# One block for norm, input projection and S5 in a hybrid Hyena, S5 and mixture-of-experts layer

## What is computed

```python
hc = modulate(rmsnorm(ctx, norm1_g[l]), csh1, csc1)
u_c = (hc @ w_in[l][:, HY_COLS:]).astype(jnp.float32)
stc_f, stc_b = s5_states(u_c, *s5_par, zero, zero)
init_f, init_b = stc_f[-1], stc_b[0]
...
h = modulate(rmsnorm(x, norm1_g[l]), sh1, sc1)
z = h @ w_in[l]
u = z[..., HY_COLS:].astype(jnp.float32)
st_f, st_b = s5_states(u, *s5_par, init_f, init_b)
y = jnp.concatenate([hyena_branch(z[..., :HY_COLS], rows, conv_w[l], conv_b[l], filt, hy_bias[l]),
                     s5_readout(u, st_f, st_b, *s5_out)], axis=-1)
x = x + g1[:, None] * (y.astype(x.dtype) @ w_out[l])
```

## Time and profile before

| | |
|---|---|
| median of 3 runs | 2789.76 us (2781.54 to 2794.0) |
| the profiled execution | 2789.57 us, span 2787.8 us |
| mean granted clock of TensorE | 0.926 |
| PE busy | 2440.3 us, 88% |
| DVE busy | 1901.2 us, 68% |
| ACT busy | 1312.9 us, 47% |
| POOL busy | 361.8 us, 13% |
| DMA | 716.41 MB, mean 257 GB/s |

### The profile page before, as it was taken

How to read it: one execution, slowest core, us unless ns; L and a number is a source line. 1 busy time by engine, 2 the same in 40 slices (tenths; PEclk the granted TensorE clock), 3 DMA queues, 4 the chain that set the end, 5 groups by cost and what they waited for, 6 DMA issues and landing times. The chain is left out here.

```text
span 2787.8 us, 27845 instructions
## 1 busy us (share of the span) xinstructions
PE 2440.3 (88%) x11074; PEld 1837.5 (66%) x11074; DVE 1901.2 (68%) x1293; ACT 1312.9 (47%) x778; POOL 361.8 (13%) x190
## 2 busy tenths in 40 slices
PE   7987499879786657749999999999999999999994
PEld 2333388633345536648888888888888888888883
DVE  4744433270729625488888888888888888888885
ACT  2111512000011122147767677777767676777673
POOL 0522300000000011000221022102201210221010
PEclk9989599999996679869999999999999999999997
DMA  7554311232235261459999999999999999999994
GB/s 255 205 191 162 99 46 31 102 117 91 90 83 120 55 204 61 172 190 360 374 368 373 378 376 371 374 373 369 380 371 375 367 376 374 379 363 376 378 363 187
DMA packets 174286, 716.41 MB, mean 257 GB/s; under 512 B 10626, under 2 KB 36130, under 8 KB 152405
## 3 DMA queue, kind: packets, MB, share of 16 engines
q1 hardware_dynamic: 167406, 689.82, 65.8%
q0 software_dynamic: 5184, 20.97, 2.8%
q10 hardware_dynamic: 1640, 4.85, 0.5%
HBM read 672.63 MB, written 42.98 MB: 257 GB/s over the span
## 5 line engine op out<-in xcount | busy, mean ns | idle before, releaser
L1819 DVE TENSOR_TENSOR w_low<-w_raw,w_high 128x4096 fp32r<-128x4096 f32 (+2 forms) x288 | 1164.0, 4064 | 93.9 <-ACT w_high L1784 93.9
L1784 ACT ACTIVATE w_high<-w_raw 128x4096 fp32r<-128x4096 f32 (+2 forms) x288 | 964.2, 3348 | 470.9 <-PE psum L1754 260.5
L1752 PE MATMUL psum<-w_high,x_high 128*128 128x512 f32 (+1 forms) x1536 | 578.4, 377 | 20.2 <-DVE w_low L1819 17.5
L1753 PE MATMUL psum<-w_low,x_high 128*128 128x512 f32 (+1 forms) x1536 | 573.8, 374 | 0.0
L1754 PE MATMUL psum<-w_high,x_low 128*128 128x512 f32 (+1 forms) x1536 | 572.1, 372 | 0.0
L1752 PEld LDWEIGHTS psum<-w_high,x_high 128*128 128x128 f32 x1536 | 290.1, 189 | 80.7 <-DVE w_low L1819 25.1
L1754 PEld LDWEIGHTS psum<-w_high,x_low 128*128 128x128 f32 x1536 | 289.3, 188 | 52.2
L1753 PEld LDWEIGHTS psum<-w_low,x_high 128*128 128x128 f32 x1536 | 289.9, 189 | 49.6
L1765 PE MATMUL psum<-w_high,a_high 128*128 128x512 f32 x704 | 220.9, 395 | 0.0
L1765 PE MATMUL psum<-w_low,a_high 128*128 128x512 f32 x704 | 217.5, 390 | 0.0
L1765 PE MATMUL psum<-w_high,a_low 128*128 128x512 f32 x704 | 217.1, 390 | 0.0
(11 more groups left out here) (321 smaller groups left out, 2835.9 us busy)
## 6 DMA issues: line engine op xcount, KB each, us to landing
w_raw<-in_ex_w_down SPq DMA_DIRECT2D x80, 2048.0 KB, 9.2
w_raw<-in_ex_w_gate SPq DMA_DIRECT2D x64, 2048.0 KB, 9.8
w_raw<-in_ex_w_up SPq DMA_DIRECT2D x64, 2048.0 KB, 10.5
w_raw<-in_ex_w_gate SPq DMA_DIRECT2D x32, 1536.0 KB, 10.3
w_raw<-in_ex_w_up SPq DMA_DIRECT2D x32, 1536.0 KB, 7.7
arena<-in_mod_w SPq DMA_DIRECT2D x24, 1024.0 KB, 7.0
w_raw<-in_ex_w_down SPq DMA_DIRECT2D x16, 1024.0 KB, 8.2
arena<-const_dft_filter SPq DMA_DIRECT2D x8, 1024.0 KB, 7.7
```

What stands on the lines that cost most here:

```text
L1752: nc.tensor.matmul(o, xt_h[:, x], h[:, f], start=kk == 0, stop=False)
L1753: nc.tensor.matmul(o, xt_h[:, x], l[:, f], start=False, stop=False)
L1784: nc.scalar.activation(high[n % NHI][:, 0:w], raw[n % NS][:, 0:w], ACT.Copy).then_inc(hi_done, 1)
L1819: nc.vector.tensor_tensor(low[n % NS][:, 0:w], raw[n % NS][:, 0:w], high[n % NHI][:, 0:w].bitcast(F32), ALU.subtract).then_inc(lo_done, 1)
```

## The change

`projection` and `s5` are replaced by one stage, `mix`, in one block. Work is cut into 36 units, one chunk by one span each; the S5 chunks 12 to 15 come first (their context spans at once, as soon as the two context tiles are there), then x1 (4 to 7), x2 (8 to 11) and v (0 to 3). Weights are loaded by chunk (512 KB, rows of 512 bytes) instead of by two chunks. Token tiles go in pairs through squares, roots and scaling, and the first five products stand between the transposes of the tokens. Four PSUM banks rotate over the units; banks 4 and 5 serve the token transposes, then the states and the turns, banks 6 and 7 the outputs. S5 has eight rounds of four columns: states of round q after unit 8 + 3q, its outputs after unit 13 + 3q. The S5 tables are reloaded in every round. The 16 turns of x1 and v follow single units; x1 and x2 go to DRAM scratch and are loaded again by `long_conv`, which also takes the broadcast rows over from `s5`. The first Fourier matrix is loaded at the end of `mix`. In `long_conv` the buffer `g` and some others lie at new addresses; the arithmetic is the same.

The diff, cut to its core:

```diff
-def projection(k):
+def mix(k):
...
+    NT, NX, NW, NZ = TOK // P, 5, 3, 3
+    NQ, A = 8, 2
+    C, G = 2 * A, 2 * A
+    chunks = [12, 13, 14, 15, 4, 5, 6, 7, 8, 9, 10, 11, 0, 1, 2, 3]
+    NCT = len(chunks)
+    units = [(n, s) for s in (2, 0, 1) for n in range(3)] + [(3, s) for s in (2, 0, 1)] + [(n, s) for n in range(4, NCT) for s in range(2)]
+    last_unit = [max(i for i, (x, _) in enumerate(units) if x == n) for n in range(NCT)]
+    ends = {i: n for n, i in enumerate(last_unit)}
+    ready = {2: 2, 0: 6, 1: NT}
+    turns = {i: [i - 15] for i in range(15, 23)}
+    turns.update({31: [8], 32: [9], 33: [10], 34: [11, 12], 35: [13, 14, 15]})
+    state_at = {8 + 3 * q: q for q in range(NQ)}
+    turn_unit = {m: i for i in turns for m in turns[i]}
+    states_done = {i: sum(s <= i for s in state_at) for i in range(len(units))}
+    turns_done = {q: sum(turn_unit[m] < i for m in turn_unit) for i, q in state_at.items()}
...
+    spans = [slice(0, 512), slice(512, 1024), slice(0, CTX)]
...
+            def put_inputs(n):
+                b = ubuf_of[n]
+                sp.wait_ge(conv, last_unit[n] + 1)
+                sp.dma_start(k.z_u[n * P:(n + 1) * P].rearrange("p s k -> p (s k)"), ubuf[b]).then_inc(uout[b], 16)
...
+            def in_tables(q):
+                if q:
+                    sp.wait_ge(smm, C * q)
+                else:
...
+                sp.dma_start(et.rearrange("p r d a n -> p (r d) (a n)"), t.rearrange("p r a n -> p r (a n)")).then_inc(tgot, 16)
...
+            def out_tables(q):
+                if q:
+                    sp.wait_ge(omm, q)
+                else:
+                    sp.wait_ge(mm, last_unit[2] + 2)
+                sp.dma_start(ot.rearrange("p r d a n -> p (r d) (a n)"), t.rearrange("p r a n -> p r (a n)")).then_inc(ogot, 16)
+                for w in range(2):
+                    for s in range(T):
+                        sp.dma_start(ll[NH * s:NH * s + NH, :, w, :], lsrc[w, :, A * q:A * q + A, (T - 1 - s) * NH:(T - 1 - s) * NH + P]).then_inc(ogot, 16)
+
+            def chunk_inputs(q):
+                if q >= 3:
+                    sp.wait_ge(omm, q - 2)
+                for s in range(T):
...
+                    sp.dma_start(uc[q % 3][NH * s:NH * s + NH, :, :], src[s, :, G * q:G * q + G, :]).then_inc(ugot[q % 3], 16)
...
+            def put_outputs(q):
+                sp.wait_ge(oev, q + 1)
+                for t in range(T):
+                    sp.dma_start(dst[t, :, G * q:G * q + G, :], ys[q % 2][NH * t:NH * t + NH, :, :]).then_inc(yput[q % 2], 16)
...
+            tokens(0)
+            tokens(1)
+            weights(0)
+            tokens(2)
+            tokens(3)
+            weights(1)
+            tokens(4)
+            weights(2)
+            for n in range(5, NT):
+                tokens(n)
+            in_tables(0)
+            for i in range(6, len(units)):
+                if i in ends and ends[i] + NW < NCT:
+                    weights(ends[i] + NW)
+                if i in ends and ends[i] < 4:
+                    put_inputs(ends[i])
+                if i == 8:
+                    sp.wait_ge(uout[0], 16)
+                    chunk_inputs(0)
+                    chunk_inputs(1)
+                if i == 9:
+                    out_tables(0)
+                if i == 11:
+                    sp.wait_ge(uout[1], 32)
+                    sp.wait_ge(uout[2], 16)
+                    chunk_inputs(2)
+                if i in state_at and state_at[i] + 1 < NQ:
+                    in_tables(state_at[i] + 1)
+                if i in output_at:
+                    q = output_at[i]
+                    if q + 3 < NQ:
+                        chunk_inputs(q + 3)
+                    if q + 1 < NQ:
+                        out_tables(q + 1)
+                    put_outputs(q)
+                if i in (17, 19, 21, 23):
+                    q = (i - 17) // 2
+                    sp.wait_ge(vev, 2 * q + 2)
+                    sp.dma_start(k.x1_d[:, :, q * P:(q + 1) * P], x1_out[:, q % 2]).then_inc(x1o[q], 16)
+                if i in (22, 24, 26, 28):
+                    q = (i - 22) // 2
+                    sp.wait_ge(conv, last_unit[8 + q] + 1)
+                    sp.dma_start(k.x2_d[:, q, :], z_t[:, (8 + q) % NZ, :]).then_inc(x2o[q], 16)
+            sp.dma_start(k.ring[:, 0, :], k.c["dft_signal"][0].rearrange("p m k n -> p (m k n)")).then_inc(pre, 16)
+            for q in range(HQ):
+                sp.wait_ge(x1o[q], 16)
+                sp.wait_ge(x2o[q], 16)
+            for b in range(2):
+                sp.wait_ge(yput[b], 16 * T * 4)
+            sp.wait_ge(pre, 16)
 
...
+            def turn_tokens(n):
                 pe.wait_ge(norm, n + 1)
                 if n >= 2:
                     pe.wait_ge(ev, n - 1)
                 for kk in range(KD):
...
+            def product(i):
+                n, s = units[i]
+                pe.wait_ge(wlo, n + 1)
+                pe.wait_ge(hlo, ready[s])
+                if i >= 4:
+                    pe.wait_ge(conv, i - 3)
...
                 last.then_inc(mm, 1)
...
+            def turn_channels(m):
+                n, r = 4 + m // 2 if m < 8 else 8 + m // 2, m % 2
+                pe.wait_ge(conv, last_unit[n] + 1)
+                pe.wait_ge(vev, m - 1 if m >= 13 else m)
+                pe.wait_ge(sev, C * NQ if m >= 11 else C * states_done[turn_unit[m]] - 1)
...
+            def states(q):
+                pe.wait_ge(tgot, 16 * (q + 1))
+                pe.wait_ge(ugot[q % 3], 16 * T * (q // 3 + 1))
+                if turns_done[q]:
+                    pe.wait_ge(vev, turns_done[q])
+                for c in range(C):
...
+                    if n >= 2:
+                        pe.wait_ge(sev, n - 1)
...
+            def outputs(q):
+                pe.wait_ge(ogot, 16 * (1 + 2 * T) * (q + 1))
+                pe.wait_ge(std, q + 1)
+                if q:
+                    pe.wait_ge(oev, q)
...
+                last.then_inc(omm, 1)
...
+            turn_tokens(0)
+            turn_tokens(1)
+            product(0)
+            turn_tokens(2)
+            product(1)
+            turn_tokens(3)
+            product(2)
+            turn_tokens(4)
+            turn_tokens(5)
+            product(3)
+            turn_tokens(6)
+            turn_tokens(7)
+            product(4)
+            turn_tokens(8)
+            turn_tokens(9)
+            for i in range(5, len(units)):
+                product(i)
+                if i in state_at:
+                    states(state_at[i])
+                if i in output_at:
+                    outputs(output_at[i])
+                for m in turns.get(i, []):
+                    turn_channels(m)
...
+            def high_part(n):
+                act.wait_ge(wgot[n % NW], 16 * (n // NW + 1))
+                if n >= NW:
+                    act.wait_ge(mm, last_unit[n - NW] + 1)
+                nc.scalar.activation(whigh[n % NW], wraw[n % NW], ACT.Copy).then_inc(whi, 1)
...
+            def middle(i):
+                n, s = units[i]
+                c = chunks[n]
+                act.wait_ge(mm, i + 1)
...
+                if 7 <= n < 11:
+                    act.wait_ge(vtr, 2 * (n - 6))
+                elif 11 <= n < 15:
+                    act.wait_ge(x2o[n - 11], 16)
+                elif n == 15:
+                    act.wait_ge(vtr, 10)
...
+            def states(q):
+                bre, bim = bu[q % 2]
+                if q >= 2:
+                    act.wait_ge(std, q - 1)
...
+                    act.wait_ge(smm, q * C + c + 1)
...
+            squares(0)
+            roots(0)
+            scaled(0)
+            scaled(1)
+            squares(1)
             high_part(0)
+            high_tile(0)
+            high_tile(1)
+            roots(1)
+            scaled(2)
+            scaled(3)
+            squares(2)
             high_part(1)
...
+            high_tile(2)
+            roots(2)
+            high_part(2)
+            high_tile(3)
+            scaled(4)
+            scaled(5)
+            squares(3)
...
+            for i in range(7, len(units)):
+                if i >= 12:
+                    middle(i)
+                if i - 1 in ends and ends[i - 1] + NW < NCT:
+                    high_part(ends[i - 1] + NW)
+                if i == 8:
+                    sines(1)
+                if i == 9:
+                    sines(2)
+                if i >= 11 and i - 11 in range(0, 15, 3):
+                    sines(3 + (i - 11) // 3)
+                if i in state_at:
+                    states(state_at[i])
+                if i in output_at:
+                    outputs(output_at[i])
+                for m in turns.get(i, []):
+                    if m >= 8:
+                        keep(m)
...
+            def low_part(n):
+                dve.wait_ge(whi, n + 1)
+                tt(wlow[n % NW], wraw[n % NW], whigh[n % NW].bitcast(F32), ALU.subtract).then_inc(wlo, 1)
...
+            def neighbours(i):
```

(77 more changed lines are left out.)

593 lines of the change are left out of this document (258 added, 335 removed).

## The result

The changed kernel takes **2706.8 us** (median of 4 runs, 2701.5 to 2709.6) beside 2789.7 us for the kernel before (median of 4): ratio 0.970, 95% interval 0.968 to 0.973. The forecast was 2711 with a range of 2690 to 2745. The profiled execution took 2701.5 us, span 2699.7; it is the fastest of its four, so the spans of the two profiles lie further apart (88.1 us) than the medians (82.9).

The account below looks back on a forecast made before the run. PE's queue plus the waits standing in it was taken as the bound of the new block: +86.8 us for the longer block, -165.5 for the S5 stage gone, -78.7 in all, from 2789.76 to 2711 us, range 2690 to 2745.

Parts of the forecast that it names:

- Startup: Token chain, early products and turns at PE's low clock: product(6) starts at 360.4 us, the block's first load being at 273.2.
- rival (e): Block start: products 0 to 3 at full clock, inputs sooner: -14 us, 2697, down to 2685; chance 0.14.
- The hole: PE waits 12 us ahead of states(0), at 388.9, for unit(8)'s write and then the first S5 input loads.
- States(0) and (1): DVE's chain and ACT's sines ahead of states(1) make PE wait; states(1) end at 415.2 us.
- The rounds: After states(1), PE's queue of products 130.6, states 29.5, outputs 48.2 and turns 7.8: 216.1 us, product(35) ends at 631.3.
- Rival (c): DVE and ACT pace the rounds through angles, sines and states: 3 us a round, 21 us, 2732; chance 0.14.
- What the matmuls cover: PE's matmuls (186 us) cover DVE's S5 work (124 us), and PE's own S5 work runs at full clock.
- (a): The SP queue paces the rounds, table loads at 0.8 us, 8 to land: +24 us, 2735; chance 0.15.
- Rival (b): SP queue paces the rounds at the old loads' full price, weights transfer ahead: +114 us, 2825; chance 0.04.
- rival (d): PE's clock doesn't hold among short matmuls; slower outputs and cold starts of units behind: +59 us, 2770; chance 0.05.
- ACT's tables: Table loads for Sin between Copy and Identity on ACT: bounds 0 and 20 us, taken as 0.
- The end: After product(35), 4.5 us of ends and a barrier of 0.9; with the matrix already loaded, the convolution starts at 636.7 us.

Follow-up runs that it names:

- e8: Changed kernel with products 0 to 4 behind the turns of all ten token tiles on PE, their copies behind DVE's evacuations: 2704.1 us.
- e2: Changed kernel with sines(q+3) moved behind the state copies of the same unit in ACT's queue: 2695.8 us.
- e9: Changed kernel with sines behind state copies, also sines(1) behind those of states(0), and first S5 input loads issued earlier, behind chunk 4's weights: 2683.3 us.
- e4: Changed kernel with six more linked 640-element instructions on DVE in each round (one product of turn_back repeated): 2733.6 us.
- e1: Changed kernel without the interleaving: all 36 products first, then the eight S5 rounds, sines behind the state copies: 2804.2 us.
- e3: Changed kernel with each s5_local load issued three times in rounds 0 to 6, the copies to unused places: 2773.0 us.
- e12: Changed kernel with each s5_local load issued twice in rounds 0 to 6: 2722.6 us.
- e11: Changed kernel without the early load of the first matrix, which the first convolution loads itself: 2710.0 us.

## Why the prediction was right, step by step

PE's queue with its waits added up as forecast where it counts most, in the rounds. The steps around them were off by up to 6.9 us, and part of that cancelled: the block was 6.9 us shorter than forecast, and the convolutions 2.0 us longer.

Counted from the first load (the prediction's times less 273.2, the measured ones less 270.2):

| step | forecast | measured |
|---|---|---|
| product(0) starts | 20.1 | 21.2 |
| product(3) starts | 59.6 | 54.5 |
| product(6) starts | 87.2 | 80.3 |
| products 6 to 8 | 16.3 | 16.6 |
| hole ahead of states(0) | 12.2 | 8.2 |
| states(0) to the end of states(1) | 26.3 | 29.1 |
| to the end of product(35) | 216.1 | 217.0 |
| to the first convolution | 5.4 | 5.4 |
| longer block | +86.8 | +79.9 |

- **Startup, 6.9 us too long.** The mis-sized term is the early products and turns. I priced products of 256 columns at 5.2 to 5.4 us, all at the low clock, and the turns behind them at 2.0. They took 4.4 to 4.6 and, behind products 0 and 1, 1.04. In product(0) the matmuls stand 0.21 us apart, then 0.12 from the middle of it on: the granted clock went from its lower level (1.2 GHz) to its upper (2.4 GHz) inside the product, and the turn behind it ran at the upper one. Product(6) came 6.9 us early, outside the 5 I had given. That is part of rival (e). e8 adds that these early products, which I followed step by step, have no effect on the end.
- **The hole, 4.0 us too long.** Write, loads and PE in series was the right mechanism. The size came from loads of 80 KB, 8.7 us from issue to PE; the new ones of 40 KB took 6.4 (368.87 to 375.27), and unit(8) was written 1.4 us after product(8) instead of 2.9. That PE falls to its low clock in it was right: states(0) took 5.1 us, at a granted clock of 0.58.
- **States(0) and (1), 2.8 us too short.** DVE's chain and the wait behind the sines were forecast, the wait was 5.1 us, and e2 confirms its cause. The chain itself, from turn_in to the end of the angles, took 18.5 us (18.8 forecast). The main term that was too small is the one put at nothing, the low clock in states(0): its copies were done 5.7 us after its start and not 3.6. In e9, where the hole is gone and states(0) ran at clock 1.00, they were done after 4.0. DVE's chain starts behind these copies, and PE waits for that chain in states(1), so PE was the late one there. The end of states(1) came 4.9 us after the angles, 3.9 forecast. States(0) in the windows view, the changed kernel and e9:

```profile
375.27:380.40 5.13, 5.13 (x49) 4.85 (x49) 0.00 (x0) 1.49 (x6) 0.00 (x0) 0.58 0.27 58
...
379.30:383.50 4.20, 4.03 (x54) 3.59 (x55) 3.96 (x9) 2.10 (x9) 0.00 (x0) 1.00 1.01 317
```

- **The rounds, right to 0.9 us in 217.** Eight outputs of 5.98 us (6.0), the clock at 0.99. Putting ACT's middle copy, high_part and sines onto PE's account was the step that made the sum come out: states 2 to 7 took 28.2 us on PE (29.5; the 1.4 us for late angles in q=4 did not come), and e2 gets just those sines back. But the sentence that DVE "fits, with little left" named the wrong slack: of the 5.1 us a round added in e4, all but about 1.5 came through as waits of PE in rounds with sines, since the loop through ACT was nearly as long as PE's queue. Rival (c) named the right engines, and by e4 most of its 3 us a round would have come through in the rounds with sines; that DVE was busy for 24.8 of 28 us said nothing against it.
- **What the matmuls cover, in part wrong.** The prediction named DVE's S5 work, and said that PE's own S5 work would run at full clock. e1 bears out the clock, but without the cover its rounds of 24 to 25 us were set by outputs and loads in series, not by DVE. The forecast didn't need this, as it added up PE's queue; the expectation of e1 did, and was 34 to 54 us too low.
- **SP, rivals (a) and (b).** They didn't happen: s5_local loads of 16 KB took 0.48 to 0.53 us of issue and a median of 1.8 us to land, where the 128 KB ones had taken 1.14 and 11.1. Rival (b) put the price that eats the whole gain at 1.1 us a load with 11.1 to land; no run has such a landing time. With 1.7 to land and 1.48 us for each table load, e3 lost 65 of the 83 us. A good part goes far sooner: at 0.94 to 1.03 us in e12 it is 17 us. The rival looked at the tables, and the weights behind them are what comes late first. The Trainium skill, "DMA: Bandwidth & Descriptors", section "Anatomy of one DMA — SWDGE (gpsimd) path", puts a fixed cost of about 2.0 us on each DMA issued from there. These went through SP, and their landing time of 1.8 us is near it; 16 of them issued in 7.6 to 8.5 us show that it overlaps, so that it counts once a round, behind the issues.
- **The clock, rival (d).** 0.90 in the round from states(1) to states(2), which holds the 5.1 us wait, and 1.00 in the five behind it. Where waits stood ahead of the short matmuls it was 0.57 and 0.64 in two rounds of e1 and 0.74 to 0.89 in five of e3, so the rival's mechanism is real and only its condition was missing.
- **ACT's tables, taken at nothing.** One table load for the sines in the whole block; Identity and Copy behind Sin cost none.
- **The end.** The convolution started 5.4 us after product(35), as forecast, and e11 prices the early load at 4.8 us there. The convolutions were 2.0 us longer in this profile than before (265.9). In the thirteen profiles with the added loads they took 265.6 to 267.9, in five of them 265.6 to 266.2, so the loads cost little or nothing there; with one profile of before, the 2.0 us can't be told from scatter.

## What to carry to other kernels

Where one engine's queue is filled with another stage's work, look in each queue at what stands ahead of a short instruction that someone waits for: here sines, a weight copy and a store's wait each cost 4 to 12 us by their place in the queue; no instruction had to be changed to get that back. Count an engine's slack up to the first thing that others wait for, including what stands behind in its queue; idle time inside a loop of engines is mostly no slack (e4), and a queue whose own consumer is served in time can still be late for the next one (e12). A merge like this can be worth nothing without the interleaving (e1), since what that hides is the loads' chain and the low clock, beside the other engine's work.

## What the runs showed of the hardware

Loads of 16 KB went through SP at 0.494 us each, 48 in a row in 23.72 us, and landed in 1.7 us each (e3, median). A wait ahead of short matmuls cost more than its length: e3 lost 65 us for 31 us of added waits, e4 26.4 us for 18.2 between states(1) and states(7). The same outputs took 6.0 us in a full queue and 10.9 us, at a granted clock of 0.50, behind a wait.
